# Norms moved into block-major output projections, and wider input loads, in an eight-core decoder trunk

## The chip, the cores and the metric

The kernel runs on all 8 cores of one Trainium2 chip (trn2). Each core handles one prompt of 2048 tokens and 16 of the 128 sample tokens, with its own copy of the work and no exchange between cores. The metric is the device time in microseconds of the slowest core. Cores 0 to 3 are one die, cores 4 to 7 the other.

## The reference

Four layers with d_model 1024. Layers 0 and 2 are "even": a causal pooling mixer and a chunked gating MLP behind one input projection. Layers 1 and 3 are "odd": a gated short convolution. Every layer then cross-attends into 256 memory tokens. There is an RMSNorm ahead of each mixer and ahead of each attention, and one at the end. Cut to what matters here:

```python
def rms_norm(x, g):
    y = xf * lax.rsqrt(jnp.mean(xf * xf, axis=-1, keepdims=True) + EPS)
    return (y * g.astype(jnp.float32)).astype(x.dtype)

for i in range(DEPTH):
    hp = rms_norm(xp, norm_mix_g[i])
    op, ... = pool_sgu_mixer(hp, ...)  or  short_conv_mixer(hp, ...)   # ends in "@ w_out"
    xp = xp + op
    kp, vp = memory_kv(mem_prompt, norm_mem_g[i], w_k[i], w_v[i])
    xp = xp + cross_attend(rms_norm(xp, norm_xattn_g[i]), kp, vp, w_q[i], w_o[i])
y_prompt = rms_norm(xp, norm_final_g)
```

The sample tokens (xs) take the same path with cached keys and values.

## The kernel before

Activations lie feature-major: `XP` [128, 8, 2064] is the residual stream in f32, with 8 feature chunks of 128 on the partitions and 2048 + 16 tokens along the row. `H` is the normed input and `YA` the mixer or attention output, both bf16. Tokens are taken in the five blocks of `BLK`: four of 512 and one of 16. `PSA` is PSUM, eight banks. Matrices come in pieces of 256 columns by `wload` through the four slots of `WB` (GpSimd's DMA queue, POOL, which also casts to bf16; slots in rotation). `TT` holds three f32 scratch rows (T0, T1, T2) of 2080, `TB` two bf16 ones.

Each instruction is recorded by class `Prog`, which keeps one list per engine in the order in which the code calls it and adds semaphore waits from the named tiles (`reads`, `writes`). Nothing is reordered: each engine executes its list from top to bottom, and so does each DMA queue, whose entry waits until its buffer is free. As every instruction is issued in `replay`, the profile shows L169 for all of them, so the groups are told apart by tiles.

- `proj` (L315) makes one 128-feature column of an output for the given blocks: eight matmuls into the next PSUM bank in rotation, then an evacuation by the caller's function.
- `rms_norm_fm` (L331) norms all of XP into H in nine steps (eight of 256 tokens and one of 16). A step is a square by ScalarE (ACT) into `TB`, eight matmuls with `onesb` into bank 4 or 5, Ln and Exp by ACT into `RS`, and eight multiplications by VectorE (DVE) into H. It is called at the head of each mixer and each attention.
- `out_proj` (L364) loops over four pieces of the weight matrix, in each over two feature columns, in each over the five blocks. `resid_add` adds the result from PSUM to XP.
- The staging loop (L373, `q8`) reads the prompt in eight loads of 1 MB, in turn into T0 and T1, and transposes each with 16 matmuls against the identity.
- `att_mem_pre` and `att_mem_pe` make keys and values of the memory tokens for a layer, with their weights through `WB`. For layer 0 they run at the start. For layers 1 to 3 they are hooks in the preceding attention's `out_proj`: the first ahead of piece 0, the second ahead of piece 2.

Around them: an even layer begins with loads into T0 to T2 on the SyncE (SP) queue, transposes of `sgu_w` and `spool`, and a mask select on POOL, and its first matmuls read four w_in_ab pieces together. An odd layer begins with 16 small transposes of `sconv` and ends with transposes of its new state. In the attention core, 16 rounds handle one prompt head and block and one sample token each, with the sample's keys and values loaded through T0 and T1.

Of the kernel before, what the change touches and what calls it, by code (L numbers as in the profile page):

```python
# [167 lines left out]
def I(method, *args, **kw):  # L168
    return lambda e: getattr(e, method)(*args, **kw)  # L169


def build_program():
# [29 lines left out]
    with ExitStack() as st:  # L202
# [49 lines left out]
        def psk(*bs):  # L252
            return [("PS", b) for b in bs]
# [38 lines left out]
        def gcol(c):  # L292
            return GV[:, c:c + 1]
# [37 lines left out]
        def rms_norm_fm(gbase, dst, dstkey, fp32_out=False):  # L331
            for bi in range(5):
                t0b, nb = BLK[bi]
                for t0 in range(t0b, t0b + nb, 256):
                    n = min(256, t0b + nb - t0)
                    p = nrm["k"] % 2
                    nrm["k"] += 1
                    sq = TBf[:, p * 2048:p * 2048 + 8 * n].rearrange("p (k n) -> p k n", k=8)
                    rs = RS[:, p * 256:p * 256 + n]
                    P.op("act", I("activation", out=sq, in_=XP[:, :, t0:t0 + n], func=AF.Square),  # L340
                         reads=[("XP", kc, bi) for kc in range(8)], writes=[SQK[p]])
                    P.group("pe", [I("matmul", PSA[:, 4 + p, 0:n], lhsT=onesb[:], rhs=sq[:, kc, :],
                                     start=(kc == 0), stop=(kc == 7)) for kc in range(8)],
                            reads=[SQK[p], "onesb"], writes=psk(4 + p))
                    P.op("act", I("activation", out=rs, in_=PSA[:, 4 + p, 0:n], func=AF.Ln, bias=EPSC[:, 0:1], scale=1.0 / D),
                         reads=psk(4 + p) + ["EPSC"], writes=[RSK[p]])
                    P.op("act", I("activation", out=rs, in_=rs, func=AF.Exp, scale=-0.5), reads=[RSK[p]], writes=[RSK[p]])
                    for kc in range(8):
                        P.op("dve", I("scalar_tensor_tensor", out=dst(kc, t0, n), in0=XP[:, kc, t0:t0 + n],
                                      scalar=gcol(gbase + kc), in1=rs, op0=ALU.mult, op1=ALU.mult),  # L350
                             reads=[("XP", kc, bi), RSK[p], "GV"], writes=[(dstkey, kc, bi)])
# [11 lines left out]

        def out_proj(wd, r0, src, srckey, hooks=None):  # L364
            for pr in range(4):
                if hooks and pr in hooks:
                    hooks[pr]()
                wv, wkey = wload(wcols(wd, r0, 8, pr * 256, 256))
                for jj in range(2):
                    fc = pr * 2 + jj  # L370
                    proj(wv, wkey, jj * 128, 8, src, srckey, resid_add(fc))

        for q8 in range(8):  # L373
            xst = TT[:, q8 % 2, 0:2048].rearrange("p (a b) -> p a b", a=2)
            xk = TK[q8 % 2]
            P.dma("sp", I("dma_start", out=xst, in_=xp_d[q8 * 256:(q8 + 1) * 256, :].rearrange("(t p) f -> p t f", p=128)),
                  writes=[xk])
            for kc in range(8):
                b = next_acc()
                P.group("pe", [I("transpose", out=PSA[:, b, t * 128:(t + 1) * 128], in_=xst[:, t, kc * 128:(kc + 1) * 128],  # L380
                                 identity=ident[:]) for t in range(2)], reads=[xk, "ident"], writes=psk(b))
                if kc % 2:
                    P.op("act", I("activation", out=XP[:, kc, q8 * 256:(q8 + 1) * 256], in_=PSA[:, b, 0:256], func=AF.Copy),
                         reads=psk(b), writes=[("XP", kc, q8 // 2)])
                else:
                    P.op("dve", I("tensor_copy", out=XP[:, kc, q8 * 256:(q8 + 1) * 256], in_=PSA[:, b, 0:256]),
                         reads=psk(b), writes=[("XP", kc, q8 // 2)])
# [10 lines left out]
        def even_layer(i):  # L398
# [42 lines left out]
            rms_norm_fm(i * 8, lambda kc, t0, n: H[:, kc, t0:t0 + n], "H")  # L441
# [168 lines left out]
            out_proj(w_out_ab_d[j], 0, YA, "YA")  # L610
# [4 lines left out]
        def odd_layer(i):  # L615
# [13 lines left out]
            rms_norm_fm(i * 8, lambda kc, t0, n: H[:, kc, t0:t0 + n], "H")  # L629
            P.op("dve", I("memset", T1[:, 0:16], 0.0), writes=[TK[1]])  # L630
            for half in range(2):
# [61 lines left out]
                out_proj(w_out_c_d[j], half * D, YA, "YA")  # L693
# [14 lines left out]
        def att_mem_pre(i):  # L708
            mnt = TBf[:, 0:2048].rearrange("p (k m) -> p k m", k=8)
            memst = T2[:, 0:2048].rearrange("p (a b) -> p a b", a=2)  # L710
            P.dma("sp", I("dma_start", out=memst, in_=mem_d.rearrange("(a p) f -> p a f", p=128)), writes=[TK[2]])
            for a in range(2):
                P.op("act", I("activation", out=TB[:, 1, 0:1024], in_=memst[:, a, :], func=AF.Square,
                                                        accum_out=VST[:, a:a + 1]),
                     reads=[TK[2]], writes=[TBALL, [("VST", 0), ("VST", 1)]])
            P.op("act", I("activation", out=VST[:], in_=VST[:], func=AF.Sqrt, bias=EPSC[:, 0:1], scale=1.0 / D),
                 reads=[[("VST", 0), ("VST", 1)], "EPSC"], writes=[[("VST", 0), ("VST", 1)]])
            P.op("dve", I("reciprocal", out=VST[:], in_=VST[:]), reads=[[("VST", 0), ("VST", 1)]], writes=[[("VST", 0), ("VST", 1)]])
            for a in range(2):
                P.op("dve", I("tensor_scalar", out=memst[:, a, :], in0=memst[:, a, :], scalar1=VST[:, a:a + 1],  # L720
                                                           scalar2=None, op0=ALU.mult),
                     reads=[TK[2], [("VST", 0), ("VST", 1)]], writes=[TK[2]])

        def att_mem_pe(i):
            mnt = TBf[:, 0:2048].rearrange("p (k m) -> p k m", k=8)
            memst = T2[:, 0:2048].rearrange("p (a b) -> p a b", a=2)
            for kc in range(8):
# [7 lines left out]
                     reads=psk(b) + ["GV"], writes=[TBALL])  # L735
            for which, (wd, od) in enumerate([(wk_d, nmk_d), (wv_d, nmv_d)]):
                for q in range(4):
                    wv_, wk_ = wload(wcols(wd[i], 0, 8, q * 256, 256))
                    for a in range(2):
# [4 lines left out]
                            reads=[TBALL, wk_], writes=psk(b))  # L744
# [7 lines left out]
                    if which == 0:  # L752
                        for jj in range(2):
# [5 lines left out]
                                reads=[TBALL, wk_], writes=psk(b))  # L759
# [7 lines left out]
        def attention(i):  # L767
            P.mute = not DBG.get("a_q", True)
            rms_norm_fm(32 + i * 8, lambda kc, t0, n: H[:, kc, t0:t0 + n], "H")
# [192 lines left out]
```

How the kernel before makes its waits and increments, by code:

```python
            def body(eng):  # L150
                for waits, fn, sig in self.ops[e]:
                    for k, v in waits:
                        eng.wait_ge(semh[k], v)
                    if fn is None:
                        continue
                    ins = fn(eng)
                    if sig is not None:
                        if sig[0] == "eng":
                            ins.then_inc(semh[sig[1]], 1)
                        else:
                            ins.then_inc(semh[sig], 16)
```

## Time and profile before

| | |
|---|---|
| time before, median of 3 runs | 3690.37 us (3687.0 to 4173.78) |
| the profiled execution's own time | 3690.01 us |
| its span, slowest core (core 7) | 3688.4 us |
| spans of all cores | 3669.8 to 3688.4 us |
| mean granted TensorE clock | 0.893 to 0.896 of 2.4 GHz |
| busy PE / DVE / ACT / POOL | 86% / 46% / 25% / 8% of the span |

PE is TensorE's matmuls, PEld its weight loads, which overlap them. The span is that of the slowest core from first to last instruction. A busy share is an average over stages that are limited in different ways, so the stages have to be read one at a time. "Idle before" of a group is the idle time of the same engine just ahead of its instructions, with what released it. PEclk is the clock that TensorE was granted: 1.00 is 2.4 GHz and 0.50 is 1.2 GHz.

### The profile page before, as it was taken

The page shows a single profiled execution, that of the slowest core. Times are in us where ns is not written, and L with a number is a line of the kernel's source. Part 1 is how long each engine was busy: PE and PEld are TensorE (multiplying, and loading weights), DVE is VectorE, ACT ScalarE, POOL GpSimd, SP SyncE. Part 2 cuts the span into 40 slices and gives each one's busy share as a digit, 9 for nine tenths or more (in the row PEclk, how much of TensorE's full clock was granted, in tenths as well). Part 3 has the DMA queues.
Part 4 walks back from the last instruction along what each step waited for, and adds up shares of the span by engine and source line. Part 5 has one row for each costly group of instructions (what it writes and reads, how often), then busy time and mean ns, then how long its engine had stood idle before and what let it go on. Part 6 is the DMA issues. An engine that isn't in the chain of part 4 may idle for free.

```text
span 3688.4 us, 51191 instructions; the slowest of 8 cores (3669.8 to 3688.4 us)
## 1 busy us (share of the span) xinstructions
PE 3171.6 (86%) x17848; PEld 1585.3 (43%) x17848; DVE 1709.4 (46%) x3610; ACT 925.1 (25%) x1588; POOL 276.7 (8%) x349
## 2 busy tenths in 40 slices
PE   4499998887799999978869999788879999997883
PEld 3274443334344444433437444333434444443332
DVE  2353465263454445435455346526354445442643
ACT  2331121431322022143233113133132212214312
POOL 1000000021000000001100000002000000000100
PEclk8699999878799999977879999887879999997796
DMA  5523223097232323327742222409713233231832
GB/s 133 98 26 39 32 38 62 9 146 101 33 37 34 46 30 40 41 42 121 104 86 30 35 33 37 70 8 152 109 13 44 30 42 37 33 48 23 132 52 92
DMA packets 258178, 213.80 MB, mean 58 GB/s; under 512 B 6772, under 2 KB 216972, under 8 KB 257770
## 3 DMA queue, kind: packets, MB, share of 16 engines
q0 software_dynamic: 244992, 173.04, 34.7%
q1 hardware_dynamic: 12938, 37.50, 3.1%
q8 instruction: 151, 2.47, 0.3%
q14 instruction: 97, 0.79, 0.1%
HBM read 366.00 MB, written 19.62 MB: 105 GB/s over the span
## 4 chain that ended last, share of the span: by engine, by line
PE 82%; ACT 5%; DMA 4%; DVE 4%; issue 4%; DVEq 0%; SPq 0%; ACTq 0%; POOLq 0%
PE PSA L169 82%; ACT TB L169 3%; DVE TT L169 2%; ACT RS L169 1%; DVE TB L169 1%; DMA WB<-w_v 1%; DMA TT<-xp 1%; ACT TT L169 0%; DMA WB<-w_o 0%; DMA WB<-w_in_ab 0%; ACT L169 0%; DMA TT<-spool 0%; DMA yp<-TT 0%; DMA TT<-mem 0%; DMA TT<-cv 0%
## 5 line engine op out<-in xcount | busy, mean ns | idle before, releaser
L169 PE MATMUL PSA<-H,WB 128*128 128x512 bf16 (+1 forms) x8704 | 1606.0, 344 | 10.9 <-DMA WB<-w_in_ab 7.0
L169 PEld LDWEIGHTS PSA<-H,WB 128*128 128x128 bf16 x8704 | 742.6, 98 | 868.5 <-issue 34.7
L169 PE MATMUL PSA<-YA,WB 128*128 128x512 bf16 (+1 forms) x3840 | 693.7, 340 | 11.8 <-DVE VST L169 7.4
L169 PEld LDWEIGHTS PSA<-YA,WB 128*128 128x128 bf16 x3840 | 323.0, 98 | 382.8 <-issue 25.4
L169 DVE TENSOR_TENSOR XP<-PSA,XP 128x512 f32<-128x512 f32 (+1 forms) x480 | 273.0, 586 | 399.1 <-PE PSA L169 399.0
L169 ACT ACTIVATE TT<-PSA 128x512 f32<-128x512 f32 (+3 forms) x339 | 190.4, 562 | 898.8 <-PE PSA L169 775.7
L169 PE MATMUL PSA<-TB,onesb 128*128 128x256 bf16 (+2 forms) x744 | 189.8, 414 | 225.6 <-ACT TB L169 217.0
L169 DVE SCALAR_TENSOR_TENSOR TB<-TT,PSA 128x256 bf16<-128x256 bf16 x512 | 215.7, 421 | 324.8 <-PE PSA L169 272.5
L169 DVE TENSOR_TENSOR TT<-PSA,TT 128x512 f32<-128x512 f32 (+1 forms) x320 | 188.3, 588 | 372.8 <-PE PSA L169 340.2
L169 ACT ACTIVATE YA<-PSA 128x512 bf16<-128x512 f32 (+1 forms) x368 | 192.9, 544 | 472.0 <-PE PSA L169 471.6
L169 DVE SCALAR_TENSOR_TENSOR H<-XP,GV,RS 128x256 bf16<-128x256 f32 (+1 forms) x576 | 217.8, 452 | 119.5 <-ACT RS L169 117.2
L169 ACT ACTIVATE TB<-XP 128x2048 bf16<-128x2048 f32 (+2 forms) x77 | 138.5, 1799 | 371.6 <-DVE XP L169 371.6
L169 PEld LDWEIGHTS PSA<-TB,onesb 128*128 128x128 bf16 x744 | 79.4, 126 | 286.9 <-issue 262.7
L169 DVE SCALAR_TENSOR_TENSOR TT<-TT,GV 128x2048 f32<-128x2048 f32 (+1 forms) x96 | 158.0, 1646 | 83.6 <-ACT TT L169 77.0
L169 PE MATMUL PSA<-ident,TT 128*128 128x128 f32 (+3 forms) x402 | 69.9, 341 | 117.8 <-DVE TT L169 43.1
L169 ACT ACTIVATE TB<-PSA 128x512 bf16<-128x512 f32 (+2 forms) x144 | 104.9, 741 | 242.8 <-PE PSA L169 242.7
L169 PE MATMUL PSA<-ES,TT 128*128 128x1 bf16 x1024 | 97.4, 164 | 69.2 <-ACT ES L169 1.3
L169 PE MATMUL PSA<-WB,H 128*128 128x256 bf16 (+1 forms) x1216 | 145.5, 278 | 1.0 <-ACT RS L169 1.0
L169 PEld LDWEIGHTS PSA<-WB,H 128*128 128x128 bf16 (+1 forms) x1216 | 117.0, 98 | 24.6 <-issue 7.9
L169 POOL DMA_DIRECT2D WB<-w_in_c x64 | 56.0, 874 | 920.0 <-PE PSA L169 920.0
L169 DVE TENSOR_TENSOR TT<-TT 128x2048 f32<-128x2048 f32 x40 | 91.7, 2293 | 69.0 <-ACT TT L169 66.5
L169 PEld LDWEIGHTS PSA<-ES,TT 128*128 128x128 bf16 x1024 | 65.2, 97 | 126.5 <-issue 126.5
(103 smaller groups left out, 1846.7 us busy)
## 6 DMA issues: line engine op xcount, KB each, us to landing
TT<-ck POOLq DMA_DIRECT2D x64, 512.0 KB, 7.9
TT<-cv POOLq DMA_DIRECT2D x64, 512.0 KB, 7.3
WB<-w_in_c POOLq DMA_DIRECT2D x64, 512.0 KB, 5.9
WB<-w_in_ab POOLq DMA_DIRECT2D x40, 512.0 KB, 5.8
WB<-w_k POOLq DMA_DIRECT2D x16, 512.0 KB, 12.6
TT<-xp SPq DMA_DIRECT2D x8, 1024.0 KB, 6.6
WB<-w_v POOLq DMA_DIRECT2D x16, 512.0 KB, 10.5
WB<-w_out_ab POOLq DMA_DIRECT2D x16, 512.0 KB, 5.7
```

Of the source, the lines that this page charges most:

```text
L169: return lambda e: getattr(e, method)(*args, **kw)
```

## The change

The norm's loop body becomes `norm_blk`, which norms one block. A new `out_proj_bm` loads all four weight pieces first and then goes block by block: eight feature columns for one block, then a hook. It replaces `out_proj` in the last output projection of each mixer and in each attention. The hook is `norm_blk` of the block just made, for the next stage. The norm stages at the heads of mixers and attentions go, but for layer 0's first one; the final norm is unchanged. In the attention's hooks the square always goes to the second half of `TB`, as the first half may hold the normed memory tokens. `att_mem_pre` runs before the blocks and `att_mem_pe` after block 1. As `WB` is full with w_o, the w_k and w_v pieces go to the two halves of T1. The prompt is staged in four loads of 2 MB into T0 and T1 together, with 32 transposes each.

```diff
+        def norm_blk(bi, gbase, fixed_p=None):
+            t0b, nb = BLK[bi]
+            for t0 in range(t0b, t0b + nb, 256):
+                n = min(256, t0b + nb - t0)
+                p = nrm["k"] % 2
+                nrm["k"] += 1
+                q = p if fixed_p is None else fixed_p
...
+        def out_proj_bm(wd, r0, src, srckey, pre=None, hooks=None):
+            ws = [wload(wcols(wd, r0, 8, pr * 256, 256)) for pr in range(4)]
+            if pre:
+                pre()
+            for bi in range(5):
+                for fc in range(8):
+                    wv, wkey = ws[fc // 2]
+                    proj(wv, wkey, (fc % 2) * 128, 8, src, srckey, resid_add(fc), blks=[bi])
+                if hooks:
+                    hooks(bi)
...
-        for q8 in range(8):
-            xst = TT[:, q8 % 2, 0:2048].rearrange("p (a b) -> p a b", a=2)
-            xk = TK[q8 % 2]
...
+        xstage = TT[:, 0:2, :].rearrange("p a b -> p (a b)")[:, 0:4096].rearrange("p (a b) -> p a b", a=4)
+        for q4 in range(4):
+            P.dma("sp", I("dma_start", 
+                out=xstage, in_=xp_d[q4 * 512:(q4 + 1) * 512, :].rearrange("(t p) f -> p t f", p=128)),
+                writes=[TK[0], TK[1]])
...
-            rms_norm_fm(i * 8, lambda kc, t0, n: H[:, kc, t0:t0 + n], "H")
+            if i == 0:
+                rms_norm_fm(i * 8)
...
-            out_proj(w_out_ab_d[j], 0, YA, "YA")
+            out_proj_bm(w_out_ab_d[j], 0, YA, "YA", hooks=lambda bi: norm_blk(bi, 32 + i * 8))
...
-                out_proj(w_out_c_d[j], half * D, YA, "YA")
+                if half == 0:
+                    out_proj(w_out_c_d[j], half * D, YA, "YA")
+                else:
+                    out_proj_bm(w_out_c_d[j], half * D, YA, "YA", hooks=lambda bi: norm_blk(bi, 32 + i * 8))
...
-                    wv_, wk_ = wload(wcols(wd[i], 0, 8, q * 256, 256))
+                    ks_ = (which * 4 + q) % 2
+                    wv_ = TT[:, 1, :].bitcast(BF16)[:, ks_ * 2048:(ks_ + 1) * 2048].rearrange("p (a b) -> p a b", a=8)
+                    wk_ = TK[1][ks_]
+                    P.dma("pool", I("dma_start", out=wv_, in_=wcols(wd[i], 0, 8, q * 256, 256)), writes=[wk_])
...
-            hooks = None
-            if i + 1 < DBG["layers"]:
-                hooks = {0: (lambda: att_mem_pre(i + 1)), 2: (lambda: att_mem_pe(i + 1))}
-            out_proj(wo_d[i], 0, YA, "YA", hooks)
+            nxt = i + 1 < DBG["layers"]
+
+            def hk(bi):
+                if nxt:
+                    if bi == 1:
+                        att_mem_pe(i + 1)
+                    norm_blk(bi, (i + 1) * 8, fixed_p=1)
+            out_proj_bm(wo_d[i], 0, YA, "YA", pre=(lambda: att_mem_pre(i + 1)) if nxt else None, hooks=hk)
```

How PE's list changes between layer 0's last output projection (`PSA<-YA,WB`) and its q projection (`PSA<-H,WB`); `PSA<-TB,onesb` are the norm's sums over the squares:

```order
-L169 MATMUL PSA<-YA,WB 128x512 x32
-L169 MATMUL PSA<-YA,WB 128x16 x8
-L169 MATMUL PSA<-TB,onesb 128x256 x64
+L169 MATMUL PSA<-YA,WB 128x512 x64
+L169 MATMUL PSA<-TB,onesb 128x256 x16
+L169 MATMUL PSA<-YA,WB 128x512 x64
+L169 MATMUL PSA<-TB,onesb 128x256 x16
+L169 MATMUL PSA<-YA,WB 128x512 x64
+L169 MATMUL PSA<-TB,onesb 128x256 x16
+L169 MATMUL PSA<-YA,WB 128x512 x64
+L169 MATMUL PSA<-TB,onesb 128x256 x16
+L169 MATMUL PSA<-YA,WB 128x16 x64
```

The first two rows stood eight times, once for each feature column, and all 64 sums of the wide blocks came behind them. Now 16 sums stand behind each block's 64 matmuls, and the narrow block has its 64 matmuls at the end.

POOL's list, which issues the weight loads, from layer 1's attention into layer 2, an even layer:

```order
-L169 DMA WB<-w_o 128x8x256 x2
-L169 DMA WB<-w_k 128x8x256 x4
-L169 DMA WB<-w_v 128x8x256 x4
-L169 DMA WB<-w_o 128x8x256 x2
+L169 DMA WB<-w_o 128x8x256 x4
+L169 DMA TT<-w_k 128x8x256 x4
+L169 DMA TT<-w_v 128x8x256 x4
 L169 AFFINE_SELECT WT<-TT 128x512
 L169 DMA WB<-w_in_ab 128x8x256 x12
```

The four w_o loads now come together, and w_k and w_v have another destination. The select and the w_in_ab loads stay behind them.

SP's list at the start, where the small vectors and the prompt are loaded:

```order
 L169 DMA TT<-conv_w 96x128
-L169 DMA TT<-xp 128x2x1024 x8
+L169 DMA TT<-xp 128x4x1024 x4
 L169 DMA OST<-xs 16x1024
 L169 DMA TT<-mem 128x2x1024
```

Eight loads became four of twice the size, in the same place.

## Rows read from the trace of the kernel before

**Rows 1.** The page: chain that ended last, by engine, share of the span.
```profile
PE 82%; ACT 5%; DMA 4%; DVE 4%; issue 4%; DVEq 0%; SPq 0%; ACTq 0%; POOLq 0%
```

**Rows 2.** Waits of PE: waiting engine, releaser, us in total, times, longest us.
```profile
PE PSA L169 <- ACT TB L169: 217.0, 72, 7.2
```

**Rows 3.** Timeline, 624 to 690 us: start us, us, engine, instruction, count, idle before.
```profile
627.02 0.69 DVE L169 TENSOR_TENSOR XP<-PSA,XP 128x512 f32<-128x512 f32 x1 [1.16 <-PE PSA L169]
...
627.86 1.91 ACT L169 ACTIVATE TB<-XP 128x2048 bf16<-128x2048 f32 x1 [67.77 <-DVE XP L169]
...
632.13 1.03 PE L169 MATMUL PSA<-TB,onesb 128*128 128x256 bf16 x8
...
633.25 1.28 ACT L169 ACT_TABLE_LOAD   x1 [3.48 <-PE PSA L169]
...
637.47 1.87 PE L169 MATMUL PSA<-TB,onesb 128*128 128x256 bf16 x8 [4.30 <-ACT TB L169]
...
642.37 1.87 PE L169 MATMUL PSA<-TB,onesb 128*128 128x256 bf16 x8 [3.03 <-ACT TB L169]
...
670.40 0.36 PE L169 MATMUL PSA<-TB,onesb 128*128 128x16 bf16 x8 [1.43 <-ACT TB L169]
...
670.63 15.70 PE L169 MATMUL PSA<-H,WB 128*128 128x512 bf16 x64
```

**Rows 4.** Stretches: length, busy us of PE, PEld, DVE, ACT, POOL; PEclk, DMA share, GB/s.
```profile
670.63:674.15 3.52, 3.52 (x14) 1.28 (x12) 3.52 (x14) 0.49 (x2) 0.00 (x0) 0.50 0.02 5
...
752.66:756.07 3.41, 2.34 (x21) 1.34 (x21) 2.70 (x13) 0.49 (x1) 0.14 (x1) 1.00 1.02 183
756.07:759.48 3.41, 3.41 (x9) 0.98 (x8) 2.02 (x6) 1.49 (x4) 1.27 (x2) 0.50 0.86 126
...
1928.17:1933.67 5.50, 5.50 (x26) 3.78 (x27) 3.65 (x15) 0.17 (x1) 0.00 (x0) 0.50 0.02 4
```

**Rows 5.** Timeline, 838 to 962 us, where layer 1 begins.
```profile
950.31 0.40 PE L169 MATMUL PSA<-ident,TT 32*128 32x32 f32 x4 [0.84 <-DVE XP L169]
...
954.44 1.86 PE L169 MATMUL PSA<-TB,onesb 128*128 128x256 bf16 x8 [0.90 <-DVE SCX L169]
```

**Rows 6.** Timeline of DVE within an output projection of layer 0's attention.
```profile
857.08 0.77 DVE L169 TENSOR_TENSOR XP<-PSA,XP 128x512 f32<-128x512 f32 x2 [1.03 <-PE PSA L169]
859.00 0.69 DVE L169 TENSOR_TENSOR XP<-PSA,XP 128x512 f32<-128x512 f32 x1 [1.16 <-PE PSA L169]
```

**Rows 7.** DMA issues, 838 to 962 us: count, KB each, median us to landing.
```profile
WB<-w_v POOLq DMA_DIRECT2D x4, 512.0 KB, 10.2
...
WB<-w_k POOLq DMA_DIRECT2D x2, 512.0 KB, 5.7
```

**Rows 8.** Timeline where layer 2 begins; DMA issues of 1885.80 to 1886.80 us.
```profile
1880.65 1.05 PE L169 MATMUL PSA<-ident,TT 128*128 128x128 f32 x8
...
1883.24 3.53 POOL L169 DMA_DIRECT2D WB<-w_in_ab  x4 [0.33 <-issue]
...
WB<-w_in_ab POOLq DMA_DIRECT2D x2, 512.0 KB, 11.1
```

**Rows 9.** The start: two stretches, PE's timeline, DMA issues of 1.0 to 5.6 us.
```profile
24.69:33.80 9.11, 2.40 (x12) 2.44 (x13) 1.39 (x4) 1.23 (x1) 0.00 (x0) 1.00 0.65 230
6.40:23.75 17.35, 0.00 (x0) 0.00 (x0) 1.69 (x5) 0.00 (x0) 2.93 (x4) 1.00 1.04 122
...
31.40 5.86 PE L169 MATMUL PSA<-ident,TT 128*128 128x128 f32 x32 [6.80 <-DMA TT<-xp]
...
65.75 0.66 PE L169 MATMUL PSA<-ident,OST 16*128 16x16 f32 x8
...
TT<-norm_mix_g SPq DMA_DIRECT2D x1, 16.0 KB, 1.7
```

**Rows 10.** Timeline of PE, layer 1's memory keys and values in layer 0's attention.
```profile
884.44 3.57 PE L169 MATMUL PSA<-WB,TB 128*128 128x256 bf16 x16 [4.15 <-DVE TB L169]
...
919.20 30.27 PE L169 MATMUL PSA<-YA,WB 128*128 128x512 bf16 x160 [3.40 <-DMA WB<-w_o]
```

More of the change, by code:

```diff
@@ L329, in build_program @@
         nrm = {"k": 0}
-        def rms_norm_fm(gbase, dst, dstkey, fp32_out=False):
-            for bi in range(5):
[L333 to L351, printed above, removed]
@@ new lines, in norm_blk @@
+        def norm_blk(bi, gbase, fixed_p=None):
[5 more added lines that the diff above has]
+                q = p if fixed_p is None else fixed_p
+                sq = TBf[:, q * 2048:q * 2048 + 8 * n].rearrange("p (k n) -> p k n", k=8)
+                rs = RS[:, p * 256:p * 256 + n]
+                P.op("act", I("activation", out=sq, in_=XP[:, :, t0:t0 + n], func=AF.Square),
+                     reads=[("XP", kc, bi) for kc in range(8)], writes=[SQK[q]])
+                P.group("pe", [I("matmul", PSA[:, 4 + p, 0:n], lhsT=onesb[:], rhs=sq[:, kc, :],
+                                 start=(kc == 0), stop=(kc == 7)) for kc in range(8)],
+                        reads=[SQK[q], "onesb"], writes=psk(4 + p))
+                P.op("act", I("activation", out=rs, in_=PSA[:, 4 + p, 0:n], func=AF.Ln, bias=EPSC[:, 0:1], scale=1.0 / D),
+                     reads=psk(4 + p) + ["EPSC"], writes=[RSK[p]])
+                P.op("act", I("activation", out=rs, in_=rs, func=AF.Exp, scale=-0.5), reads=[RSK[p]], writes=[RSK[p]])
+                for kc in range(8):
+                    P.op("dve", I("scalar_tensor_tensor", out=H[:, kc, t0:t0 + n], in0=XP[:, kc, t0:t0 + n],
+                                  scalar=gcol(gbase + kc), in1=rs, op0=ALU.mult, op1=ALU.mult),
+                         reads=[("XP", kc, bi), RSK[p], "GV"], writes=[("H", kc, bi)])
@@ L378, in build_program @@
             for kc in range(8):
                 b = next_acc()
[L380 to L384, printed above, removed]
-                else:
-                    P.op("dve", I("tensor_copy", out=XP[:, kc, q8 * 256:(q8 + 1) * 256], in_=PSA[:, b, 0:256]),
-                         reads=psk(b), writes=[("XP", kc, q8 // 2)])
+                fns = [I("transpose", out=PSA[:, b, t * 128:(t + 1) * 128],
+                                                              in_=xstage[:, t, kc * 128:(kc + 1) * 128],
+                                                              identity=ident[:]) for t in range(4)]
@@ new lines, in build_program @@
+                P.group("pe", fns, reads=[TK[0], TK[1], "ident"], writes=psk(b))
+                eng = "act" if kc % 2 else "dve"
+                if eng == "act":
+                    P.op("act", I("activation", out=XP[:, kc, q4 * 512:(q4 + 1) * 512],
+                                                                         in_=PSA[:, b, :], func=AF.Copy),
+                         reads=psk(b), writes=[("XP", kc, q4)])
+                else:
+                    P.op("dve", I("tensor_copy", out=XP[:, kc, q4 * 512:(q4 + 1) * 512],
+                                                                          in_=PSA[:, b, :]),
+                         reads=psk(b), writes=[("XP", kc, q4)])
@@ L712, in att_mem_pre @@
             for a in range(2):
-                P.op("act", I("activation", out=TB[:, 1, 0:1024], in_=memst[:, a, :], func=AF.Square,
+                P.op("act", I("activation", out=TBf[:, 0:1024], in_=memst[:, a, :], func=AF.Square,
                                                         accum_out=VST[:, a:a + 1]),
-                     reads=[TK[2]], writes=[TBALL, [("VST", 0), ("VST", 1)]])
+                     reads=[TK[2]], writes=[SQK[0], [("VST", 0), ("VST", 1)]])
             P.op("act", I("activation", out=VST[:], in_=VST[:], func=AF.Sqrt, bias=EPSC[:, 0:1], scale=1.0 / D),
@@ L768, in attention @@
             P.mute = not DBG.get("a_q", True)
-            rms_norm_fm(32 + i * 8, lambda kc, t0, n: H[:, kc, t0:t0 + n], "H")
+            if not DBG["mix"]:
+                rms_norm_fm(32 + i * 8)
             for pr in range(4):
```

13 lines of the change are left out of this document (7 added, 6 removed).

## The prediction

> **What bounds the kernel now.** I read the page's chain first: TensorE (PE) carries 82% of it [rows 1]. Everything outside PE matters only where PE waits for it, so the table of PE's waits came next. Its first line is ScalarE's squares: 217 us in 72 waits, far ahead of any other releaser [rows 2]. All but a few of these stand in the eight RMSNorm stages, so I then read the timeline of one of them, the norm between layer 0's mixer and its q projection.
>
> The reader should see a strict ping-pong in it [rows 3]. ScalarE squares half a block (1.9 us), PE sums it with eight matmuls on the ones matrix (1.87 us), ScalarE makes the reciprocal root, and only then squares the next half. PE idles 3.03 us in each turn and a turn takes 642.37 - 637.47 = 4.90 us. The first square (627.86) is hidden beside the last output projections, and the first ones group runs at once, in 1.03 us. The whole stage, from the last projection at 632.1 to the first q matmul at 670.63, takes 38.5 us. Then PE runs 3.52 us at a granted clock of 0.50 (1.2 GHz) before it gets 1.00 (2.4 GHz). At half speed half of this is lost, and other stages are alike, up to 5.50 us [rows 4]. I take 4.4 us at the low level, a loss of 2.2 us for each such return to dense work, with 1.75 and 2.75 as bounds from the shortest and longest of these rows. One stage costs 38.5 + 2.2 = 40.7 us.
>
> **Part 1, the fused norm (7 of 8 stages).** The order shows where the ones matmuls now stand: right behind the eight projections of their own block, ahead of the next block's. PE takes matmuls in that order, so the next block can't cover them. For each of the four 512-token blocks PE pays:
> - The last projection must be added to XP and squared before the ones group may start. From a projection's end past its XP add to the next PE work is 0.84 us [rows 5]. The square behind it adds 1.91 us and about 0.15 us from the add to its start (627.71 to 627.86, [rows 3]), with 0.1 for the longer handover to PE: 3.0 us. Before, this was hidden beside work of other blocks.
> - The ones group 1.03 us, the gap to the second half's group 3.03 us, and that group at the low clock 1.87 us [rows 3].
>
> Together 8.9 us against 2 x 4.90 = 9.8 before: what is gained is the reciprocal root of each second half and the H writes, about 0.9 us per block. Against it stands the clock. The gaps no longer come in one stretch but four times. I take a fall in each, since in the sample attention loop the level falls to 0.50 although PE is busy 2.34 of 3.41 us just ahead of it [rows 4]. So there are four returns to dense work, 4 x 2.2 = 8.8 us, where there was one.
>
> The 16-token block now stands last and alone. Before, its eight matmuls stretched the pace of the XP adds from 0.69 + 1.03 to 0.77 + 1.16 us, by 0.2 us for each of the eight feature columns, 1.5 us in all [rows 6]. At the low clock eight such matmuls take 0.36 us [rows 3], 2.9 us in all: +1.4. Its own norm adds about 1.2 us (add, a short square, 0.36). One table load of 1.28 us stays on the path [rows 3]. Stage after: 4 x 8.9 + 8.8 + 1.4 + 1.2 + 1.28 = 48.3 us, 7.6 more than before.
>
> The weights were prefetched during the norm stage. Block-major order holds all four WB slots until the last block, and the next stage's first load can be issued only after a quarter of its 64 narrow matmuls. A load takes 5.7 us [rows 7]; 2.2 us of matmuls and the 1.2 us norm cover part: 2.4 us wait. In the q projections of layers 0 and 2 this is open. In the other four (odd layers in, odd layers out) transposes of 4.1 us and more stand between and hide it (950.31 to 954.44, [rows 5]). That gives 4 x 7.6 + 2 x 10.0 = 50.4 us. In two of the stages before an odd layer the next block's first group takes the PSUM bank that the logarithm (0.5 us) is still reading: 6 times 0.7 = 4 us.
>
> Layer 2 is worse. Its first group needs four w_in_ab loads, which stand in POOL's queue behind the mask select, which waits for the transposes after the norm. From those (1880.65) to the issue is 2.6 us, and the third and fourth load land a median 11.1 us after their own issue [rows 8]. The fourth is the later of the two by some 0.9 and is issued 2.6 us behind the first, so it lands 14.6 us after the first issue: 17.2 us in all. Before, from 1880.65 to 1928.17 plus a return of 2.2 are 49.7 us. After, 48.3 + 17.2 = 65.5: +15.8. Part 1 is 50.4 + 4 + 15.8 = **+70 us**.
>
> The Trainium skill, "TensorE: Matmul & The Clock Gate", section "HAM oscillation", warns of a loop whose bursts are parted by waits: it pays the change of clock in every turn, not once. By that rule the sum stands as above; without the three extra returns per stage it would be 46 us lower.
>
> **Part 2, input staging.** Before, 1 MB loads alternated between two buffers, and 24.69 to 65.75 took 41.1 us. Now a 2 MB load fills both, and the next one waits for all transposes. The first two loads together are the nearest thing: 230 GB/s over 9.11 us are 2.1 MB [rows 9]. 32 transposes take 5.86 us, and the wider copies out of PSUM run beside them. A round is 9.1 + 5.8 + 0.2 = 15.1 us, four are 60.4: +19.3. Against that, the first weight loads leave the start: w_k now goes into T1 and must wait. They keep the DMA engines full (share 1.04) while three tiny loads take 17.35 us [rows 9]; an undisturbed one takes 1.7 us, so I take 5.5 for three: -11.8. Bounds: 0 to -12.
>
> The page "DMA: Bandwidth & Descriptors" of the Trainium skill, section "Anatomy of one DMA", fits a fixed 2 us plus the bytes at 436 GB/s, an estimate of 6.8 us for 2 MB. By it the staging would lose 10 us and not 19. The measured pair took 9.1 us, and the measurement decides.
>
> **Part 3, memory keys and values (at the start and in three layers).** Before, from the first K matmul (884.44) to the return of the projections (919.20) are 34.8 us, a wait of 3.40 us for w_o among them [rows 10]. After, w_o is there, but w_k and w_v have two buffers and not four. Sixteen matmuls take 3.57 us at the low level and so 1.8 at the full one. K needs 32 and V 16 per load, and a load is back 5.7 us after its buffer is free [rows 7]. K: 5.8 (the clock rises on the way) + 3.5 + a wait of 2.5 + 3.5 + 3.5 = 18.8 us. V: bound by loads, (5.7 + 0.2 + 1.9)/2 = 3.9 each, 15.8 in all, 34.6 together. The write of the keys (nmk) shares the DMA engines with the V loads. With w_v's measured landing of 10.2 us [rows 7] V would take 4 x 6.1 = 24, so the bounds are 0 and +8. I take **+5**, three times 15. At the start, where no wait for w_o is there to be saved, I take +7.
>
> **Sum.** 70 + (19.3 - 11.8 + 7 = 14.5) + 15 = +99.5 us on the profiled execution's 3690.0 us, which lies 0.4 below the median shown: **3790 us**, 2.7% slower.
>
> **Rivals.**
> - *The clock holds through the gaps.* Each stage then saves 8.8 of returns, 4 x 0.84 on the ones groups and 1.4 on the narrow block, 13.6 us; seven times 95. Time 3695 us. For it: 3.03 us gaps with matmuls between them are short. Against: the loop of [rows 4], with shorter gaps, falls each turn.
> - *The norm does hide (faster).* If TensorE ran the next block's projections while a ones group waits, a stage would keep only its last blocks, about 10 us, and save 28: 3690 - 7 x 28 + 29.5 = 3523 us. It decides wherever a matmul starts between an XP add and the ones group behind it. Nothing in the trace shows a matmul that overtakes a waiting one.
> - *Loads at their upper bounds (slower still).* A 2 MB load at twice the 6.7 us of the first 1 MB one (24.69 to 31.40, [rows 9]) adds 4.3 us four times, and V at 10.2 us landing adds 3 us four times: 3790 + 29 = 3819 us.
>
> **How the numbers follow.** My forecast holds 0.63, with its own range of 3755 to 3815 us; the clock rival 0.17, the upper bounds 0.16, the hidden norm 0.04. Two per cent, about what a measurement of this kernel can tell from no change, is 74 us: above 3764 is slower. Most of the forecast (0.56) and all of the upper bounds lie there: slower 0.72. The clock rival and the forecast's lower edge give same 0.24. Faster is the hidden norm, 0.04. The range runs from within the clock rival to beyond the upper bounds: 3705 to 3840 us, leaving out about 0.2.
>
> **What would show it.** Between two blocks of a fused projection PE should idle about 3.0 us twice with one ones group between, the first released by ScalarE's square, and projections after it should run some 4 us at clock 0.50. PE's total wait for squares should stay near or above 217 us. Before w_in_ab of layer 2 there should be a wait of some 8 to 10 us on a DMA. The last input transpose should end 7 to 8 us later than now. Wrong would be a granted clock of 1.00 through the blocks, projections that run during a square, or a first xp load still issued at 24 us.

## The result and the profile after

| | before | after |
|---|---|---|
| time, median (of 3 executions before, of 10 after) | 3690.37 us | 3835.06 us |
| ratio to before | 1 | 1.0389 [1.0377, 1.0401] |
| slowest core's span | 3688.4 us (core 7) | 3835.3 us (core 2) |
| spans of all cores | 3669.8 to 3688.4 us | 3792.8 to 3835.3 us |
| mean granted clock | 0.893 to 0.896 | 0.881 to 0.889 |

The changed kernel is 3.9% slower, 144.7 us by the medians. In some executions of every kernel the cores of one die or both get a lower clock and take some per cent longer; ratios and intervals here leave those out. The forecast was 3790 us, with a range up to 3840: the direction was right and the time lies in the range, but 45 us of the loss were not in the sum.

The chain that ended last, of the kernel after (shares of the span by engine; compare [rows 1]):

```profile
PE 80%; DMA 6%; ACT 5%; DVE 5%; issue 4%; DVEq 0%; ACTq 0%; SPq 0%; POOL 0%; POOLq 0%
```

PE's waits after (released by, us in total, times, longest; compare [rows 2]):

```profile
PE PSA L169 <- ACT TB L169: 255.0, 79, 7.3
PE PSA L169 <- DVE TT L169: 49.1, 8, 9.0
PE PSA L169 <- DMA TT<-w_v: 49.0, 13, 5.8
PE PSA L169 <- DMA TT<-xp: 41.4, 4, 11.4
...
PE PSA L169 <- DMA WB<-w_in_ab: 15.9, 3, 10.5
...
PE PSA L169 <- DMA TT<-w_k: 15.1, 6, 4.1
...
PE PSA L169 <- ACT RS L169: 7.3, 11, 0.7
...
PE PSA L169 <- DMA WB<-w_q: 1.5, 2, 0.8
```

Squares rose from 217 to 255 us of waiting. The second row stood there before as well (48.1 us). What grew behind them are the waits for w_v and w_k, 64 us together where the weights of the memory keys and values cost 16.3 us (w_v) before. The waits for input loads doubled, from 20.2 to 41.4 us. The DMA share of the chain rose from 4% to 6%.

To find where the 145 us lie, I cut both traces at the same places of PE's timeline and compared the slowest cores. An "x" stage runs from a mixer's last output projection to the first q matmul, an "a" stage from an attention's output projection to the next mixer's first matmul on H:

| stretch (us) | before, core 7 | after, core 2 | change | change, mean of 8 cores | forecast |
|---|---|---|---|---|---|
| start to layer 0's first H matmul | 178.1 | 209.9 | +31.8 | +23.3 | +14.5 |
| x of layers 0 / 1 / 2 / 3 | 96.2 / 102.2 / 94.5 / 102.0 | 104.5 / 110.5 / 102.1 / 111.2 | +33.4 | +33.6 | +35.2 |
| a of layers 0 / 1 / 2 | 145.3 / 145.7 / 145.5 | 171.8 / 177.3 / 166.5 | +79.1 | +77.1 | +50.0 |
| all the rest | 2678.9 | 2681.5 | +2.6 | +0.4 | 0 |
| whole span | 3688.4 | 3835.3 | +146.9 | +134.5 | +99.5 |

The column of means cuts all eight cores of both traces at the same places. It matters because the slowest core after the change is not a typical one: it lies 22 us above the mean of its eight, where the slowest core before lay 10 us above. The forecast column regroups the terms of the prediction: x is 10.0 + 7.6 + 10.0 + 7.6; a is 7.6 + 2 + 5, then 15.8 + 5, then 7.6 + 2 + 5.

PE's timeline in the x stage of layer 0, after (start, us, operation, count, idle before it and its releaser; compare [rows 3]). `PSA<-YA,WB` are projections, `PSA<-TB,onesb` the norm's sums:

```profile
604.37 13.98 PE L169 MATMUL PSA<-YA,WB 128*128 128x512 bf16 x64
621.46 1.03 PE L169 MATMUL PSA<-TB,onesb 128*128 128x256 bf16 x8 [3.11 <-ACT TB L169]
626.80 1.87 PE L169 MATMUL PSA<-TB,onesb 128*128 128x256 bf16 x8 [4.30 <-ACT TB L169]
628.46 16.13 PE L169 MATMUL PSA<-YA,WB 128*128 128x512 bf16 x64
647.65 1.03 PE L169 MATMUL PSA<-TB,onesb 128*128 128x256 bf16 x8 [3.05 <-ACT TB L169]
...
676.12 1.87 PE L169 MATMUL PSA<-TB,onesb 128*128 128x256 bf16 x8 [3.02 <-ACT TB L169]
677.78 15.38 PE L169 MATMUL PSA<-YA,WB 128*128 128x512 bf16 x64
...
701.93 2.14 PE L169 MATMUL PSA<-YA,WB 128*128 128x16 bf16 x64
707.88 0.36 PE L169 MATMUL PSA<-TB,onesb 128*128 128x16 bf16 x8 [3.81 <-ACT TB L169]
708.86 16.86 PE L169 MATMUL PSA<-H,WB 128*128 128x512 bf16 x64 [0.61 <-DMA WB<-w_q]
```

The same projections took 13.98 us ahead of the first gaps and 16.13 behind them. The windows of the second block (PE, PEld, DVE, ACT, POOL busy, then PEclk, DMA share, GB/s) show why:

```profile
628.46:632.00 3.54, 3.54 (x10) 1.30 (x9) 2.15 (x6) 0.89 (x2) 0.00 (x0) 0.50 0.00 0
632.00:644.50 12.50, 12.50 (x57) 5.41 (x55) 5.86 (x10) 0.00 (x0) 0.00 (x0) 0.97 0.00 0
```

PE was fully busy in both, at a granted clock of 0.50 for the first 3.5 us.

What ScalarE does in the first gaps of that stage, from its timeline:

```profile
619.30 1.91 ACT L169 ACTIVATE TB<-XP 128x2048 bf16<-128x2048 f32 x1 [29.32 <-DVE XP L169]
622.58 1.28 ACT L169 ACT_TABLE_LOAD   x1 [1.37 <-PE PSA L169]
```

The first square is released by the residual add and starts 0.95 us after PE's last projection ended (604.37 + 13.98 = 618.35); PE waits for it. Before the change this square was done beside other work.

The input staging, PE's timeline from the start (compare [rows 9]):

```profile
11.37 0.59 PE L169 MATMUL PSA<-ident,TT 120*128 120x120 f32 x2 [11.37 <-DMA TT<-conv_w]
22.12 5.20 PE L169 MATMUL PSA<-ident,TT 128*128 128x128 f32 x32 [10.16 <-DMA TT<-xp]
...
70.42 6.62 PE L169 MATMUL PSA<-ident,TT 128*128 128x128 f32 x32 [10.25 <-DMA TT<-xp]
```

The four 2 MB loads took 9.9, 11.0, 9.3 and 9.9 us from issue to landing, and PE waited through each. The first one was issued at 12.1 us and no longer at 24.7.

Memory keys and values in the a stage of layer 0, after (`PSA<-TT,TB` is a matmul on a weight in T1; compare [rows 10]):

```profile
934.27 3.57 PE L169 MATMUL PSA<-TT,TB 128*128 128x256 bf16 x16 [4.32 <-DVE TB L169]
...
948.33 3.57 PE L169 MATMUL PSA<-TT,TB 128*128 128x256 bf16 x16 [4.12 <-DMA TT<-w_k]
951.69 2.88 PE L169 MATMUL PSA<-TB,TT 128*128 128x256 bf16 x16
954.41 1.91 PE L169 MATMUL PSA<-TT,TB 128*128 128x256 bf16 x16
...
962.13 3.57 PE L169 MATMUL PSA<-TT,TB 128*128 128x256 bf16 x16 [4.06 <-DMA TT<-w_v]
969.06 6.12 PE L169 MATMUL PSA<-TT,TB 128*128 128x256 bf16 x32 [3.37 <-DMA TT<-w_v]
979.87 3.57 PE L169 MATMUL PSA<-TT,TB 128*128 128x256 bf16 x16 [4.69 <-DMA TT<-w_v]
```

From the first K matmul to the end of the last V group are 979.87 + 3.57 - 934.27 = 49.2 us, where 34.8 stood before with a wait for w_o among them. This core has the longest such section of layer 0: the eight cores took 42.5 to 49.2 us, 44.9 in the mean, and 32.1 in the mean before without the wait for w_o. Four waits for weights add up to 16.2 us, and the 16 matmuls behind a wait take 3.57 us, while undisturbed ones take 1.91.

Layer 2's start, after (compare [rows 8]):

```profile
2016.15 1.89 PE L169 MATMUL PSA<-ident,TT 128*128 128x128 f32 x8
...
2034.32 9.47 PE L169 MATMUL PSA<-WB,H 128*128 128x256 bf16 x64 [10.52 <-DMA WB<-w_in_ab]
```

### The profile page after: what moved, and what is told of

Its sections match the earlier page's. It is cut to its first block, busy times and chain, and to the rows that moved or that the text cites. A ratio compares the mean times of both kernels' runs of the same rounds, so it can differ in the third digit from the quotient of the medians.

```text
span 3835.3 us, 51099 instructions; the slowest of 8 cores (3792.8 to 3835.3 us)
## 1 busy us (share of the span) xinstructions
PE 3216.4 (84%) x17848; PEld 1602.1 (42%) x17848; DVE 1704.1 (44%) x3594; ACT 923.5 (24%) x1572; POOL 276.7 (7%) x349
## 4 chain that ended last, share of the span: by engine, by line
PE 80%; DMA 6%; ACT 5%; DVE 5%; issue 4%; DVEq 0%; ACTq 0%; SPq 0%; POOL 0%; POOLq 0%
PE PSA L169 80%; ACT TB L169 3%; DVE TT L169 2%; DMA TT<-w_v 2%; DVE TB L169 1%; ACT RS L169 1%; DMA TT<-xp 1%; DMA TT<-w_k 1%; DMA WB<-w_in_ab 1%; DVE XP L169 1%; ACT TT L169 0%; DVE H L169 0%; ACT L169 0%; DMA TT<-spool 0%; DMA WB<-w_q 0%
## 5 line engine op out<-in xcount | busy, mean ns | idle before, releaser
L169 PE MATMUL PSA<-YA,WB 128*128 128x512 bf16 (+1 forms) x3840 | 725.6, 349 | 13.6 <-DVE VST L169 7.4
L169 PEld LDWEIGHTS PSA<-YA,WB 128*128 128x128 bf16 x3840 | 331.1, 101 | 403.4 <-issue 65.2
L169 PE MATMUL PSA<-TB,onesb 128*128 128x256 bf16 (+2 forms) x744 | 177.7, 391 | 256.1 <-ACT TB L169 255.0
L169 PE MATMUL PSA<-TT,TB 128*128 128x256 bf16 x512 | 91.5, 356 | 79.6 <-DMA TT<-w_v 49.0
L169 PEld LDWEIGHTS PSA<-ident,TT 128*128 128x128 f32 (+3 forms) x402 | 66.7, 195 | 142.5 <-issue 141.4
```

## The experiments

Two questions were open. For the norm: is the loss the place of the sums in PE's list, and how much of it is the clock? For the rest: what do two buffers for w_k and w_v cost, and what the wide loads? All runs below were compared with the kernel before; "in us" is the ratio times 3690.4 us, in which the kernel after is 3834 us. The interval of a ratio is worth 4 to 8 us to each side. The dummy matmuls of e2 are added work; no experiment leaves work out.

**e1: the norm's sums inside the next block's projections.** In `out_proj_bm` of the kernel after:

```
-            for bi in range(5):
+            prev = None
+            for bi in (4, 0, 1, 2, 3):
                 for fc in range(8):
                     ...
-                if hooks:
-                    hooks(bi)
+                    if nb and prev is not None and fc in (3, 7):
+                        norm_half(prev, fc // 4, *nb)
+                if mem and bi == 1:
+                    mem()
+                prev = bi
+            if nb:
+                norm_half(3, 0, *nb)
+                norm_half(3, 1, *nb)
```

`norm_half` is one step of `norm_blk`, with its sum in a bank of the projections' rotation in place of bank 4 or 5.

> Changed kernel, but each block's norm is recorded inside the next block's projections (first half after four feature columns, second half after eight), the narrow block goes first, and the sums take PSUM banks in rotation. Theory (PE pays because the sums stand right behind their own block): only block 3's norm stays open, so a fused stage falls from 102 to 105 us to about 77 us, and the time by 7 x 27 us to about 3645 us. Rival (the cost is in the block-major order, the weight loads or the clock, not in the place of the sums): the stage stays near 100 us and the time within 20 us of 3835 us.

Measured: 0.9937 [0.9916, 0.9958], 3667 us, 167 us below the kernel after. PE's timeline in the x stage of layer 0:

```profile
619.05 13.97 PE L169 MATMUL PSA<-YA,WB 128*128 128x512 bf16 x64
632.86 1.04 PE L169 MATMUL PSA<-TB,onesb 128*128 128x256 bf16 x8
633.73 7.07 PE L169 MATMUL PSA<-YA,WB 128*128 128x512 bf16 x32
```

No idle time stands before a sum until the last block's, and the projections keep their full pace (7.07 us for 32). The wait for squares fell from 255.0 to:

```profile
PE PSA L169 <- ACT TB L169: 94.1, 30, 7.0
```

The x stages of layers 0 and 1 took 76 to 80 and 86 to 88 us over the cores, where the kernel before had 96 and 102. So block-major order can hide the norm; what it needs is other work of PE recorded between an add and the sum over its square. That the change puts none there is shown as the cause of the loss in these stages. Two things came with the edit. The narrow block goes first, but in this stage it takes 13.4 us there (605.60 to 619.05) and 6.9 at the end in the kernel after, so the gain does not come from it. And the sums take their banks in rotation, which was not tried alone; the waits for `RS` that it can remove are 7.3 us in all. The time is 22 us above what was expected.

**e2: dummy matmuls in the gaps.** Twelve 512-column matmuls on `onesb` ahead of each sum, into the bank that the sum then overwrites. They read only YA, so they run during the square. The order stays as in the kernel after.

```
+                if fill and n == 256:
+                    P.group("pe", [I("matmul", PSA[:, 4 + p, :], lhsT=onesb[:], rhs=YA[:, d_, 0:512], ...
```

> Changed kernel with 12 matmuls of 512 columns (about 2.6 us at full clock) ahead of each sum of a fused norm, into the bank that the sum then overwrites, so that TensorE works through most of each 3.0 us gap; outputs are unchanged. Theory (each gap costs a fall of the clock): granted clock 1.00 through the blocks, the second sum 1.03 and not 1.87 us, a block's projections 14.0 and not 15.0 to 16.2 us; 28 blocks by 2.3 us, time about 3770 us. Rival (the clock is not what the gaps cost): no gain or a small loss, 3835 to 3850 us.

Measured: 1.0271 [1.0254, 1.0288], 3790 us, 44 us below the kernel after, although PE does more. The timeline of the same stage, and the window of its second block:

```profile
637.67 2.75 PE L169 MATMUL PSA<-YA,onesb 128*128 128x512 bf16 x12
640.89 1.03 PE L169 MATMUL PSA<-TB,onesb 128*128 128x256 bf16 x8 [0.47 <-ACT TB L169]
641.76 2.75 PE L169 MATMUL PSA<-YA,onesb 128*128 128x512 bf16 x12
645.06 1.03 PE L169 MATMUL PSA<-TB,onesb 128*128 128x256 bf16 x8 [0.54 <-ACT TB L169]
645.93 13.98 PE L169 MATMUL PSA<-YA,WB 128*128 128x512 bf16 x64
```

```profile
623.86:637.67 13.81, 13.81 (x66) 6.23 (x64) 8.25 (x17) 0.89 (x2) 0.00 (x0) 1.00 0.00 1
```

The clock holds at 1.00, the second sum takes 1.03 us and no longer 1.87, and a block 13.98. This isolates the clock's part of the norm term, but for what the filler itself costs. In this stage the narrow block's sum comes 8.0 us sooner after the first projection: 5.2 from three blocks at full pace and 4 x 0.84 = 3.4 from the second sums, less 0.5 for filled second gaps of 3.14 us and not 3.02. The wait for w_q behind it then takes 3.1 us back (3.69 on this core and 0.61 on the core shown after), and the return behind the narrow block is still there. Over all stages 44 us are 6.3 per stage, where 65 us had been expected in all.

**e3: the old staging in the kernel after.** Eight loads of 1 MB, in turn into T0 and T1; everything else as after.

```
-        for q4 in range(4):
-            P.dma("sp", I("dma_start", 
-                out=xstage, in_=xp_d[q4 * 512:(q4 + 1) * 512, :].rearrange("(t p) f -> p t f", p=128)),
-                writes=[TK[0], TK[1]])
+        for q8 in range(8):
+            xst = TT[:, q8 % 2, 0:2048].rearrange("p (a b) -> p a b", a=2)
+            xk = TK[q8 % 2]
```

> Changed kernel with the input staging of before (eight 1 MB loads in two buffers); w_k and w_v stay in T1. Theory (the single wide buffer costs about 24 us and hides the 12 us that the freed start gives): the last prompt transpose ends near 53 us and not 69 to 77 us, time about 3813 us. Rival (the wide load itself is harmless, and the loss at the start is in the weights through T1): time within 5 us of 3835 us.

Measured: 1.0336 [1.0319, 1.0353], 3814 us, 20 us less. The staging ends with:

```profile
54.12 1.94 PE L169 MATMUL PSA<-ident,TT 128*128 128x128 f32 x16 [0.70 <-DMA TT<-xp]
```

That ends at 56 us, and at 77 in the kernel after. All of the gain is there: in the mean of the eight cores the first H matmul comes 20.7 us sooner.

**e6: the wide staging alone, in the kernel before** (the same edit the other way round).

> Kernel before with only the input staging of the change (four 2 MB loads in one buffer), memory weights still in WB and loaded at the start. Theory (each wide load lies open, the first still issued at about 24 us): the last prompt transpose ends near 85 us, time +22 us, about 3711 us. Rival (fewer, larger loads cost nothing): within 5 us of 3690 us.

Measured: 1.0036 [1.0023, 1.0049], 3704 us: +13 us, where the forecast has +19.3 for the rounds. PE reached the first transposes of the input at:

```profile
32.04 5.22 PE L169 MATMUL PSA<-ident,TT 128*128 128x128 f32 x32 [10.50 <-DMA TT<-xp]
```

That is ten microseconds later than after (22.12), because here the w_k loads still go first. So the 12 us that the start gained are not a gift of the wide loads; they come from the four w_k loads that had to leave, and e3 keeps them too. The staging ended at 77 to 88 us over the cores, 61 to 69 before the change: at the start the loss was some 17 us. In the mean of the cores 4.5 us of it come back in the a stages, which the edit leaves alone; e8 leaves them alone too and has them 5.6 us shorter, so this looks like a difference between the traces and not like an effect of the edit. Nothing here settles it.

**e4: a third buffer for w_k and w_v**, the second half of TB, which is free while keys and values are made:

```
-                    ks_ = (which * 4 + q) % 2
+                    ks_ = (which * 4 + q) % 3
...
+                    else:
+                        wv_ = TBf[:, 2048:4096].rearrange("p (a b) -> p a b", a=8)
+                        wk_ = SQK[1]
```

> Changed kernel with three buffers for w_k and w_v and not two (T1's halves and the second half of TB). Theory (the sections on memory keys and values wait for a load's turn round): each of the four sections loses 6 to 8 us of waits, time about 3808 us. Rival (the DMA engines' rate, or the write of the keys beside the loads, sets the pace): no gain, within 5 us of 3835 us.

Measured: 1.0255 [1.0235, 1.0276], 3784 us: 50 us less, twice what I expected. The end of the section in the a stage of layer 0:

```profile
945.77 3.44 PE L169 MATMUL PSA<-TB 128*128 128x256 bf16 x16 [2.61 <-DMA TB<-w_v]
951.83 5.32 PE L169 MATMUL PSA<-TT,TB 128*128 128x256 bf16 x32 [2.61 <-DMA TT<-w_v]
```

It ends at 957.2 after a first K matmul at 925.77, so 31.4 us and not 49.2. With three buffers no wait for w_k is left there and only two for w_v. In the mean of the cores the four sections are 9.8, 12.2, 13.5 and 10.4 us shorter, 46 of the 50 us. Each buffer wait costs twice: the wait itself, and the low clock behind it. The expectation had counted the waits alone.

**e5: block-major order without the fused norm**, all norms back at the heads (memory weights and staging as after):

```
-            if i == 0:
-                rms_norm_fm(i * 8)
+            rms_norm_fm(i * 8)
...
-            out_proj_bm(w_out_ab_d[j], 0, YA, "YA", hooks=lambda bi: norm_blk(bi, 32 + i * 8))
+            out_proj_bm(w_out_ab_d[j], 0, YA, "YA")
...
```

> Changed kernel with block-major projections, but the norms back in one stretch at the heads of mixers and attentions. Theory (the fused norm itself costs some 8 us per mixer stage and 10 to 12 in the attention stages, besides the loads): the stages around the cross-attention norms return to 95 to 97 and 102 us, the time falls by about 75 us to 3760 us; what is left over 3690 us is staging and memory weights. Rival (block-major order costs by itself, through its 16-token block and held weight slots): at most half of that gain, 3800 us or more.

Measured: 1.017 [1.0152, 1.0188], 3753 us, 81 us less than after. The x stages are back at 95 and 102 us, as before the change, and the norm has its old form:

```profile
656.45 1.87 PE L169 MATMUL PSA<-TB,onesb 128*128 128x256 bf16 x8 [4.30 <-ACT TB L169]
```

Block-major order as such costs nothing in these stages. Undone one at a time, the fused norms give 81 us back, the memory buffers 50 and the staging 20: 151 us, against the 144 between the kernels. They add up within their intervals.

**e8: the fused norm of the four mixers alone, in the kernel before.** The four calls of `out_proj_bm` with its hook replace the old projection and the norm ahead of the attention; attention, memory and staging stay as before.

> Kernel before with the change's fused norm only in the last output projection of each mixer (the four cross-attention norms); attention, staging and memory weights as before. Theory (8.3 us lost in each such stage, as the two traces show): four stages, +33 us, about 3723 us. Rival (a stage's loss comes from what the other edits do to the DMA engines): within 10 us of 3690 us.

Measured: 1.0074 [1.0052, 1.0096], 3718 us, so +27 us or 6.8 per stage, where the forecast had 8.8 on average. The interval is worth 8 us to each side, and in the trace of one execution (3724.7 us) the four stages are 36 us longer in the mean of the cores, 9.0 each. It is the part with the least trouble around it: no layer 2 and no memory weights. The wait for w_q on the slowest core was longer than in the kernel after (3.24 us and 0.61):

```profile
681.91 8.25 PE L169 MATMUL PSA<-H,WB 128*128 128x512 bf16 x30 [3.24 <-DMA WB<-w_q]
```

**e7 and e9: e1, e3 and e4 together.** One kernel, run under two labels.

> The three repairs together: norms recorded inside the next block's projections, staging in eight 1 MB loads, three buffers for w_k and w_v. Theory (three separate costs): 3666 us less 22 less about 44, some 3600 us, 2.4% below the kernel before. Rival (the repairs share one gain, since all free the same DMA engines or gaps): 3640 us or more.

The first label has a single comparable time, 3592.7 us, and so no interval. I ran the same kernel again.

> The kernel with the three repairs once more, unchanged, for an interval: about 3593 us as its undisturbed executions before, 2.6% below the kernel before. Rival (that time was one of a lucky few executions): 3640 us or more.

Measured: 0.9752 [0.9733, 0.9771], 3599 us: 2.5% faster than the kernel before and, by the two ratios, 6.1% faster than the kernel after. The three repairs alone gained 167, 20 and 50 us, 237 in all, and together 235. The tail of a stage shows what is still open:

```profile
632.93 1.04 PE L169 MATMUL PSA<-TB,onesb 128*128 128x256 bf16 x8
637.10 1.03 PE L169 MATMUL PSA<-TB,onesb 128*128 128x256 bf16 x8 [3.13 <-ACT TB L169]
641.26 1.86 PE L169 MATMUL PSA<-TB,onesb 128*128 128x256 bf16 x8 [3.13 <-ACT TB L169]
```

Only the last block's two halves still wait for their squares, 3.13 us each. Before, seven gaps of 3.0 to 4.3 us stood in such a stage [rows 3].

## Why the prediction was right, and where a term was off

**The norm term held, in mechanism and nearly in size.** The prediction built a fused block from a gap of 3.0 us, a sum of 1.03, a gap of 3.03 and a sum of 1.87. The rows show 3.11 or 3.05, 1.03, 3.02 and 1.87. The table load of 1.28 us stands in one gap per stage (4.30). The x stages lost 33.4 us and the forecast was 35.2; e8 alone, where nothing else is changed, gave 27. The bank wait of 0.7 us before an odd layer was there as described, but eight times and not six, as the narrow block meets it too. In the a stage of layer 0, for example:

```profile
912.40 15.80 PE L169 MATMUL PSA<-YA,WB 128*128 128x512 bf16 x64 [0.71 <-ACT RS L169]
...
1012.73 1.87 PE L169 MATMUL PSA<-TB,onesb 128*128 128x256 bf16 x8 [3.06 <-ACT TB L169]
```

The second row shows what the prediction did not have: in the two a stages before odd layers most first sums of the later blocks run at the low level as well (1.87 us and not 1.03). Without their memory sections the three a stages lost 40 us in the mean of the cores, where the norm's terms for them are 35.

**Four returns to full clock per stage: right, at slightly less than 2.2 us.** The blocks of the x stage in layer 0 took 16.13, 15.63 and 15.38 us, 2.15, 1.65 and 1.40 more than 13.98, and the first 64 q matmuls 16.86, 2.9 more. That is 8.1 us where the prediction had 8.8; two of the four lie below my lower bound of 1.75. e2, which changes the clock and nothing else of the order, shows that the fall is real: the rival in which the clock holds is refuted by the rows at 0.50, and e2 is what it would have looked like. The section "HAM oscillation" of "TensorE: Matmul & The Clock Gate" in the Trainium skill says that a loop whose bursts are parted by waits pays the change of clock each turn. The trace agrees: 3.54 us at 0.50 behind a pair of gaps.

**The narrow block at the end: a wait was left out.** Its 64 matmuls took 2.14 us, not 2.9, and its sum came 3.81 us behind them, against a sum of add, short square and 0.36 of 1.2 us. VectorE's list shows why:

```profile
703.32 3.26 DVE L169 SCALAR_TENSOR_TENSOR H<-XP,GV,RS 128x256 bf16<-128x256 f32 x8 [1.64 <-ACT RS L169]
706.50 0.73 DVE L169 TENSOR_TENSOR XP<-PSA,XP 128x16 f32<-128x16 f32 x8
```

The narrow block's adds stand behind the eight multiplications of block 3's second half, and run only when these are done, 2.4 us after the narrow matmuls ended (704.07). The wait for w_q then was 0.61 us in this stage (0.8 at most on this core), not 2.4: the same time shows up as square and not as load. On the eight cores it was 0.6 to 4.0 us. In e2 and e8 the slowest core had 3.69 and 3.24. The forecast for matmuls, norm and wait together (2.9 + 1.2 + 2.4 = 6.5 us) compares with 708.86 - 701.93 = 6.93: the total is right partly by luck, as the matmuls and the wait were taken too large and the norm too small.

**Layer 2's wait for w_in_ab: right.** A wait of 8 to 10 us was forecast and 10.52 measured. From the transposes at 2016.15, which answer to those at 1880.65 [rows 8], to the first H matmul are 18.2 us, against a forecast of 17.2: the first load was issued at 2020.1 and the last landed at 2034.1.

**Staging: right in the mean, too small for the slowest core.** A 2 MB load was taken at 9.1 us, from the rate of the first two loads together. On core 2 the four took 9.3 to 11.0, 10.0 on average, and the copies out made a round longer. From the first issue (12.1) to the end (77.0) are 65 us, not 60.4, and the last transposes ended 11.2 us later than before, where I had written 7 to 8. In the mean of the eight cores it is 60.5 us (55.7 to 64.9), and the end came 8.0 us later. The first load at 12 us was forecast and came. "DMA: Bandwidth & Descriptors", "Anatomy of one DMA", in the Trainium skill would have it at 6.8 us per load. Its fit is for loads issued by GpSimd, and these are issued on SP's queue; the measurement decides, and it lies farther from that than my estimate.

**Memory keys and values: the term that was mis-sized.** Part 3 allowed 5 us for each of three layers and 7 at the start. The a stage of layer 0 took 49.2 us for it and not 34.8 (+14.4); the start took 45.9 us from the first K matmul at 89.1 to the last V, before 31.5 (+14.4 too). In the mean of the cores the four sections, from the first K matmul to the last V, are 12.9, 12.8, 13.5 and 10.7 us longer, 50 us together, where the forecast had 22. e4 gets 50 us back with one more buffer. Two steps of the working failed. First, the clock. I let it rise once, in the first K groups. But each wait for a load is a gap of 3.4 to 4.7 us, and 16 matmuls behind one take 3.57 us and not 1.91: 5.0 us in three groups, 1.0 in the one behind the first of them (2.88) and 2.5 in the group of 32, some 8 us that the sum lacked. Second, the pace of the V loads, which I took as (5.7 + 0.2 + 1.9)/2 = 3.9 us each. From 962.13 to 979.87 three steps took 17.7 us, 5.9 each, and that is the bound that stood in my own text (6.1), not the value that I chose. K took 23.8 us against 18.8 forecast, and V with its first wait 25.4 against 15.8. A smaller slip is the wait for w_o, saved in each layer by the sum: it was 3.40 us on core 7 in layer 0 [rows 10] and at most 0.9 us on any core in layers 1 and 2.

**What no term had.** Behind the memory section at the start stands a wait for sgu_w on the SP queue:

```profile
162.04 1.09 PE L169 MATMUL PSA<-ident,TT 128*128 128x128 f32 x4 [27.04 <-DMA TT<-sgu_w]
```

It was 19.6 us before. Over the eight cores it is 17.4 to 27.0 us after (21.5 in the mean) and was 18.0 to 20.2 before (18.9); its two loads landed 8.2 us after their issue in the median on core 2, and 4.0 on core 1. With the old staging (e3) and with three buffers (e4) the means are 19.6 and 19.3 us. The slowest core paid the longest wait, and with it 31.8 us at the start, against 23.3 in the mean. No experiment separates what makes a core's loads late, so that stays open.

Summed on the slowest cores: start 31.8 - 14.5 = 17.3 us too low, a stages 79.1 - 50.0 = 29.1 too low, x stages 1.8 too high. That is the 45 us between 3790 and 3835; the 2.6 us of the rest are the rest of the spans' difference. In the means of the cores the change is 134.5 us, 35 more than forecast. The memory sections hold 28 of these, the rest of the a stages 5 and the wait for sgu_w 2.6. The other 12 us are the slowest core's distance from the mean, which grew and for which the prediction had no term.

The measured time lies outside the 3755 to 3815 us of my main forecast and above the third rival (3819 us), which was nearer to it; the whole range holds it by 5 us. So the direction and the paths are right by the working, but that the range reached so far is its margin, not a term. A small slip of sum is in the working too: the narrow block stretched an add from 1.72 to 1.93 us [rows 6], eight times 0.21, which is 1.7 us and not 1.5.

## What to carry to other kernels

Here a fused reduction saved nothing as long as each sum stood right behind its own block in the list of the one engine that does both the projections and the sums. Write the sum into that engine's list behind other work that is ready (here half a block later, 167 us), and only then does fusion pay. When buffers are taken from a prefetch to make room for another, count the waits that this leaves, and for each of them the slow clock behind it as well as the wait. A wider load that fills both halves of a double buffer is no longer double buffering: the transposes of one load then hide none of the next one's time (e3 and e6: 20 and 13 us).

## What the runs showed of the hardware

- Behind two gaps of 3.0 us with eight short matmuls (1.03 us) between them, the granted clock was 0.50 in the first 3.5 us of dense work. The same place with 2.75 us of dummy matmuls in each gap, and about 0.5 us left idle, stayed at 1.00 (e2), and adding 12 matmuls per gap made the kernel 44 us faster.
- Cores that do the same work drift apart: their spans differ by 18.6 us before, by 42.5 after, by 23.0 in e4 and by 25.4 in e9. The largest difference stands where most waits for loads are exposed; that these make it is argued and not shown.
- Four 512 KB weight loads in another queue (POOL's) held up tiny loads on SP's. Where they are gone, the first input load behind six tiny ones is issued at 12.1 us and not at 24.7. The width of the input loads does not matter for that: it is about 12 us in e3 too, with the old staging, and 21 to 23 us in e6, with the wide loads and the weight loads at the start.
